# A hybrid decoder layer on one core: block pairs on unscaled operands, silu on ScalarE, fewer plain tiles, and a reordered last attention step

## The reference

```python
def rmsnorm(x, g):
    y = xf * lax.rsqrt(jnp.mean(xf * xf, axis=-1, keepdims=True) + RMS_EPS)
    return y * g

def swiglu(x, w_gate, w_up, w_down):            # D_MODEL 1024, D_FF 2816
    return (jax.nn.silu(x @ w_gate) * (x @ w_up)) @ w_down

h = h + 0.5 * swiglu(rmsnorm(h, ffn1_norm), ffn1_w_gate, ffn1_w_up, ffn1_w_down)
u = rmsnorm(h, mix_norm)
proj = u @ w_in        # pool input, q (16 heads of 64), k, v (2 heads), two gates
branch_pool = causal_pool_mixer(xp, pool_w, pool_scale) @ w_pool_out
branch_attn = sliding_window_sink_attention(q, k, v, q_norm, k_norm, sinks) @ w_attn_out
h = h + (gate_pool * branch_pool + gate_attn * branch_attn) @ w_out
h = h + 0.5 * swiglu(rmsnorm(h, ffn2_norm), ffn2_w_gate, ffn2_w_up, ffn2_w_down)
```

## Time and profile before

| what | value |
|---|---|
| median of 3 runs | 1023.11 us (1022.58 to 1025.37) |
| profiled execution, its own time | 1023.9 us |
| profiled execution, span from first to last instruction | 1022.1 us |
| granted TensorE clock, mean | 0.998 of full |
| busy: PE, PE weight load, DVE, ACT, POOL | 1015.0, 903.1, 758.1, 506.1, 309.9 us |
| matmuls | 6164 |

### The profile page before, as it was taken

How to read it: one execution, slowest core, us unless ns; L and a number is a source line. 1 busy time by engine, 2 the same in 40 slices (tenths; PEclk the granted TensorE clock), 3 DMA queues, 4 the chain that set the end, 5 groups by cost and what they waited for, 6 DMA issues and landing times.

```text
span 1022.1 us, 15961 instructions
## 1 busy us (share of the span) xinstructions
PE 1015.0 (99%) x6164; PEld 903.1 (88%) x6164; DVE 758.1 (74%) x1157; ACT 506.1 (50%) x878; POOL 309.9 (30%) x192
## 2 busy tenths in 40 slices
PE   9999999999999999999999999999999999999998
PEld 7888999998989888778888878888899999988897
DVE  6998677569986688537788766769885776599763
ACT  6543555555533343447787733336254555465231
POOL 1300233421131453444454443520014233310311
PEclk9999999999999999999999999999999999999999
DMA  6734667713332442222211222316467677233333
GB/s 216 219 106 121 178 175 190 212 45 124 94 95 103 139 139 83 83 88 65 75 62 62 83 83 63 122 41 198 111 170 202 158 183 191 90 104 104 103 104 104
DMA packets 42296, 124.86 MB, mean 122 GB/s; under 512 B 4336, under 2 KB 5616, under 8 KB 42224
## 3 DMA queue, kind: packets, MB, share of 16 engines
q1 hardware_dynamic: 37616, 107.85, 32.7%
q0 software_dynamic: 4320, 15.73, 8.7%
q10 hardware_dynamic: 288, 0.29, 0.1%
HBM read 121.76 MB, written 2.10 MB: 121 GB/s over the span
## 4 chain that ended last, share of the span: by engine, by line
PE 96%; DVE 1%; ACT 1%; DMA 1%; SPq 0%; issue 0%; DVEq 0%; ACTq 0%
PE psum L663 18%; PE psum L665 18%; PE psum L664 18%; PE psum L773 10%; PE psum L775 10%; PE psum L774 10%; PE psum L936 3%; PE psum L935 3%; PE psum L934 3%; PE psum L1090 1%; DMA h<-x_dram 1%; DVE sum_of_squares L1900 1%; PE psum L1120 1%; PE psum L1103 1%; PE psum L1121 1%
## 5 line engine op out<-in xcount | busy, mean ns | idle before, releaser
L1193 ACT ACTIVATE w_high<-w_raw 128x1024 fp32r<-128x1024 f32 x118 | 124.5, 1055 | 162.9 <-DMA w_raw<-weights_dram 113.8
L1757 POOL TENSOR_TENSOR w_low<-w_raw,w_high 128x1024 fp32r<-128x1024 f32 x50 | 122.9, 2462 | 116.5 <-ACT w_high L1193 95.5
L1757 POOL TENSOR_TENSOR w_low_in_place<-w_raw,w_high 128x1024 fp32r<-128x1024 f32 x27 | 66.4, 2461 | 196.9 <-ACT w_high L1193 196.9
L663 PE MATMUL psum<-u_high,w_high 128*128 128x512 f32 x240 | 96.9, 404 | 0.0
L665 PE MATMUL psum<-u_high,w_low 128*128 128x512 f32 x240 | 93.7, 391 | 0.0
L664 PE MATMUL psum<-u_low,w_high 128*128 128x512 f32 x240 | 93.5, 390 | 0.0
L663 PE MATMUL psum<-ffn_u_high,w_high 128*128 128x512 f32 x222 | 86.6, 390 | 0.0
L663 PE MATMUL psum<-hidden_high,w_high 128*128 128x512 f32 x222 | 86.5, 389 | 0.0
L664 PE MATMUL psum<-hidden_low,w_high 128*128 128x512 f32 x222 | 86.5, 389 | 0.0
L665 PE MATMUL psum<-ffn_u_high,w_low_in_place 128*128 128x512 f32 x222 | 86.4, 389 | 0.0
L664 PE MATMUL psum<-ffn_u_low,w_high 128*128 128x512 f32 x222 | 86.4, 389 | 0.0
(11 more groups left out here) (346 smaller groups left out, 3201.3 us busy)
## 6 DMA issues: line engine op xcount, KB each, us to landing
w_raw<-weights_dram SPq DMA_DIRECT2D x118, 512.0 KB, 3.5
gate_a<-weights_dram SPq DMA_DIRECT2D x15, 512.0 KB, 6.2
gate_s<-weights_dram SPq DMA_DIRECT2D x15, 512.0 KB, 3.7
gate_s<-weights_dram POOLq DMA_DIRECT2D x15, 512.0 KB, 6.4
up_a<-weights_dram SPq DMA_DIRECT2D x15, 512.0 KB, 4.7
up_s<-weights_dram SPq DMA_DIRECT2D x15, 512.0 KB, 3.6
up_s<-weights_dram POOLq DMA_DIRECT2D x15, 512.0 KB, 8.4
gate_a<-weights_dram SPq DMA_DIRECT2D x15, 256.0 KB, 5.2
```

Of the source, the lines that this page charges most:

```text
L663: pe.matmul(o, wh, xh, start=start, stop=False)
L1193: act.activation(high[:, s, :], raw[:, s, :], ACT.Copy).then_inc(high_done, 1)
L1757: pool.tensor_tensor(wlow[:, s, :], raw[:, s, :], high[:, s, :], ALU.subtract).then_inc(low_done, 1)
```

## The change

Four edits.

1. `PLAIN` goes from `(8, 6)` to `(6, 4)`: 6 plain tiles and 8 pairs in the first FFN, 4 and 9 in the second. The DMA of the first pair's weights is issued at other plain units.
2. The pairs work on unscaled operands. Four of the seven moving operands are now slices of the high and low parts that the plain tiles use, so their copies disappear; ACT makes `h * gain` in float32 (`unscaled`) and DVE the four sums from it (`sum_moving`). In return the results of a pair are multiplied by `rinv` on DVE: three instructions per pair that take gate and up together (`both`).
3. silu is one ACT instruction in place of tanh on ACT and two multiplications on DVE. The factor 0.25 of the residuals becomes 0.5.
4. In attention's last step DVE and ACT do `turned_part` of the last step ahead of `attn_part` of the step before it, and ACT does `small_part` ahead of the gate. POOL's last `low_part` waits for another semaphore.

```diff
-PLAIN = (8, 6)
+PLAIN = (6, 4)
-SUM_BANK = (1, 4, 3)
+SUM_BANK = (1, 4, 1)
...
+            def unscaled(n, c):
+                act.activation(ub[:, c:c + 1, :], h[:, c:c + 1, :], ACT.Identity, scale=at(gains[2 * n], c)
+                               ).then_inc(u_scaled, 1)
...
@@ ACT, pair @@
-                act.wait_ge(part_summed, 6 * g + 4)
-                act.activation(th[:, 0, :], gate_t[:, 0, :], ACT.Tanh, scale=0.5).then_inc(pair_tanh, 1)
+                act.wait_ge(pair_scaled, 3 * g + 1)
+                act.activation(gate_t[:, 1, right], gate_t[:, 1, right], ACT.Silu, scale=-1.0).then_inc(pair_silu, 1)
+                act.wait_ge(pair_scaled, 3 * g + 2)
+                act.activation(gate_t[:, 0, :], gate_t[:, 0, :], ACT.Silu).then_inc(pair_silu, 1)
                 if more:
                     high_s2(g + 1, up_w)
                     act.wait_ge(product, done(n, i, 10))
                     high_s31(g + 1, up_w)
-                act.activation(th[:, 1, right], gate_t[:, 1, right], ACT.Tanh, scale=-0.5).then_inc(pair_tanh, 1)
-                act.wait_ge(product, done(n, i, 12))
-                act.activation(th[:, 1, left], psum[:, x, left], ACT.Tanh, scale=-0.5).then_inc(pair_tanh, 1)
+                act.wait_ge(pair_scaled, 3 * g + 3)
+                act.activation(gate_t[:, 1, left], gate_t[:, 1, left], ACT.Silu, scale=-1.0).then_inc(pair_silu, 1)
...
@@ DVE, second_tile (the wait and the two multiplications by tanh are gone) @@
+                dve.wait_ge(product, done(n, i, 13))
+                dve.tensor_tensor(both[:, :, 1, left], psum[:, x:x + 2, left], two_of(rinv[:, left]), ALU.mult
+                                  ).then_inc(pair_scaled, 1)
...
@@ DVE, pair @@
                 add_part(up[:, 1, right], x + 1, 10, 6)
+                dve.wait_ge(part_summed, 6 * g + 5)
+                dve.tensor_tensor(both[:, :, 1, right], both[:, :, 1, right], two_of(rinv[:, right]), ALU.mult
+                                  ).then_inc(pair_scaled, 1)
                 add_part(up[:, 0, right], 7, 11, 5)
+                dve.wait_ge(part_summed, 6 * g + 6)
+                dve.tensor_tensor(both[:, :, 0, :], both[:, :, 0, :], two_of(rinv[:, :]), ALU.mult
+                                  ).then_inc(pair_scaled, 1)
                 if more:
                     low_s2(g + 1, up_w)
                     low_s31(g + 1, up_w)
-                dve.wait_ge(pair_tanh, 3 * g + 1)
-                dve.scalar_tensor_tensor(out=gate_t[:, 0, :], in0=th[:, 0, :], scalar=1.0, in1=gate_t[:, 0, :],
-                                         op0=ALU.add, op1=ALU.mult).then_inc(pair_silu, 1)
...
+                dve.wait_ge(pair_silu, 3 * g + 2)
                 dve.tensor_tensor(hid[:, f, :], gate_t[:, 0, :], up[:, 0, :], ALU.mult).then_inc(pair_hidden, 1)
...
@@ POOL @@
-                    pool.wait_ge(attn_low, 4 * NB)
+                    pool.wait_ge(pt_low, turned_lows(nb, j) + 3)
                     low_part(U_GATE + SLOTS + SLOTS * nb + j, j)
...
@@ DVE, norm: the sums of the moving blocks stand between its parts @@
+            norm_split(2)
+            sum_moving(1, NT2)
+            norm_variance(2)
+            sum_moving(1, T3)
+            norm_root(2)
```

More of the change, by code:

```diff
@@ L135 @@
 NEW1, NEW3, NEW2, NEW4 = range(4)
-B21, B22, B11, B12 = range(4)
-NT2, NT1, T3, T4 = range(4)
+B11, B12, B21, B22 = ((kh, half) for kh in range(2) for half in range(2))
+NT1, NT2, T3, T4 = range(4)
 def layer_kernel(nc, x_in, consts_in, params_in, poolw_in, weights_in, out):
@@ L1314, in plain @@
                     next_unit(base + 5)
-                    gate_tanh_tile(1, F)
-                    block_high(n, B22)
+                    gate_silu_tile(3, F)
                     next_unit(base + 6)
+                    high_a1(g, gate_w)
+                    high_s2(g, gate_w)
                     next_unit(base + 7)
-                    gate_tanh_tile(2, F)
-                    next_unit(base + 8)
-                    for t, count in sums[0]:
-                        sum_high(n, t, count)
@@ L1529, in _ @@
                 square(0, c, c)
+            for c in range(HALF):
+                unscaled(0, c)
             high_of_sum(0)
@@ L1742, in _ @@
                     square(2, c, c)
+                    unscaled(1, c)
             high_of_sum(2)
@@ L1907, in residual_of @@
             def residual_of(c):
[L1908 removed]
+                return dve.scalar_tensor_tensor(out=tile(h, c), in0=psum[:, c, :], scalar=0.5, in1=tile(h, c),
                                                 op0=ALU.mult, op1=ALU.add)
@@ L2055, in plain @@
+                    plain_tile(1)
                     weight_sums(g, gate_w)
                     low_a1(g, gate_w)
+                    unit_low(base + 6)
+                    sum_low(n, T3)
+                    sum_low(n, T4)
+                    low_s2(g, gate_w)
+                    unit_low(base + 7)
+                    low_s31(g, gate_w)
+                    plain_tile(2)
+                else:
+                    plain_scaled(n, base, 0, F)
+                    unit_low(base + 7)
+                    plain_scaled(n, base, 1, F)
+                    sum_moving(n, NT2)
+                    plain_hidden(0, F)
+                    plain_hidden(1, F)
+                    sum_moving(n, T3)
+                    sum_moving(n, T4)
+                    unit_low(base + 8)
+                    plain_scaled(n, base, 2, F)
+                    sum_low(n, NT1)
+                    sum_low(n, NT2)
+                    plain_hidden(2, F)
```

302 lines of the change are left out of this document (120 added, 182 removed).

## The result

The changed kernel takes **1031.87 us** (median of six executions, 1030.20 to 1034.33) against 1023.48 for the kernel before (six executions, 1022.58 to 1026.24). The ratio is 1.0079, with a 95% interval of 1.0059 to 1.0098: 0.8% slower, and 1.9 us above the predicted 1030.0. The profiled execution is the shortest of the six, 1030.2 us with a span of 1028.4 us, 6.3 us longer than the span of before.

The account below looks back on a forecast made before the run. The prediction took PE (busy 1015.0 of 1022.1 us) as the bound. From the profiled 1023.9: - 3.2 (PE work) - 3.8 (attention) + 13.9 (pairs' loop) = 1030.8, median 0.8 lower: 1030.0 us; range 1015.5 to 1035.

Parts of the forecast that it names:

- The work on PE, -3.2: In each FFN, two plain tiles (21.76 us) become one pair (20.16 us): 2 x 1.60 = 3.2 us less.
- The attention, -3.8: At the attention's end, the reorder removes PE's 2.14 us wait and slow matmuls behind it: 3.8 us less.
- A + 9.5 for the copy: In a pair, ACT's copy for the next pair's product 4 starts 9.5 us after A, the third add's start.
- The loop of 21.3: In the pairs, add, scalings, silu, copy, POOL, sums and next add close in 21.3 us against PE's 20.16; chance 0.58.
- the first sum now ends at A + 16.1, and from its end to the next third add are 5.23: In a pair, DVE's first weight sum ends behind POOL's rows, 16.1 us after the third add; 5.23 us of DVE work follow.
- the issue order: In the pairs, DVE's first sum may slip in ahead of POOL's last row, shortening the loop by about 0.1 us.
- Pair 0 has A = start + 16.1 in FFN 1: In FFN 1, pair 0's third add starts 16.1 us after the pair's start; in FFN 2, 14.9.
- the prediction's own formula: Last pair's product 4: 16.1 + 6 x 21.3 + 9.9 against 7 x 20.16 + 5.7 in FFN 1; FFN 2 likewise.
- 13.9: Total time lost to the loop in the pairs, in us: 7.0 in FFN 1 and 6.9 in FFN 2.
- The rival of the clock: In the pairs, the loop's waits also lower the clock: 22 us more, 1052 us, held unlikely; part of it 0.05.
- The plain parts at nothing: In the plain parts, plain matmuls cover the added DVE and ACT work: no cost, otherwise up to 1.2 us or twice that per FFN.

Follow-up runs that it names:

- Experiment 1: Changed kernel with ScalarE's rounding of the up weights' s2 and s31 moved ahead of the two silus within a pair; 1024.60 us.
- experiment 5: Changed kernel with GpSimd's four rows per pair copying the high part instead of subtracting, which makes those low parts wrong; 1024.11 us.
- experiment 6: Changed kernel with a pair's second scaling cut from 1024 to 32 elements a partition, so the first tile's results are not scaled; 1020.52 us.
- experiment 4: Changed kernel with two extra copies of h on ScalarE ahead of the first product's copy, in each pair but an FFN's first; 1041.98 us.
- Experiment 3: Changed kernel with ScalarE's rounding of the second down weights moved from behind to ahead of the last pair's last silu; 1026.79 us.
- experiment 8: Changed kernel with both ScalarE orders, those of Experiment 1 and Experiment 3, together; 1018.66 us.
- experiment 2: Changed kernel with ScalarE's rounding of s4 and a22 moved ahead of a pair's last silu, so GpSimd's four rows start earlier; 1035.06 us.

## Why the prediction was right, and where it was off

- **The result and its main cause: right.** The loop through scalings, silu, copy, POOL and the sums closes above PE's 20.16, and this makes the kernel slower. Experiments 1, 5 and 6 each shorten one member of it, on three different engines, and nearly all of the slip goes; experiment 4 lengthens it, and the slip grows with 0.77 of the delay.
- **The work on PE, -3.2: right** to 0.1 (21.75 and 21.76 for the plain tiles).
- **The attention, -3.8: right** in the stage (3.84) and by undoing it (418.52) or doing it alone (414.68). By the medians it is 3.0 and 3.5; the 1.7 us of it that are the clock are lost in only some executions.
- **A + 9.5 for the copy: right** (9.48), with silu at 0.63 and the scalings where they were put.
- **The loop of 21.3: mis-sized.** The step that failed is "the first sum now ends at A + 16.1, and from its end to the next third add are 5.23". POOL's last row is indeed the bound, but it holds the *second* sum: the first slips in ahead of it. The second ends at A + 16.5 with 4.5 to go: 21.0, not 21.3. In every second or third pair more of the sums slips in earlier, and the pair takes 20.7. I had allowed 0.1 for the issue order; it is 0.3 to 0.6.
- **When the loop takes hold: mis-sized.** "Pair 0 has A = start + 16.1 in FFN 1" came from the kernel before. Measured, the third add of pair 0 is 11.75 behind the issue of its `gate_a`, start + 14.8, so FFN 1 lost only what a loop entered 1.3 later loses. With 14.8 and third adds that stand 21.01 and 21.05 apart on average in the two FFNs, the prediction's own formula gives 4.0 and 5.1 us, the measured 9.1 in place of **13.9**.
- **The down projections: missed, +5.1.** The sum ended with the last pair's product 4. In a pair I had followed what stands behind each instruction that now waits longer, but not for the last silu of the *last* pair: behind it on ACT stand the second down weights, and ahead of what it waits for stand four low parts on DVE. Experiment 3 shows it. The two errors nearly cancelled (-4.8 and +5.1): that the time came out within 1.9 us is luck, though the direction is not.
- **The rival of the clock** did not come true in the pairs: the short waits left it at 1.00. It came true at the unforeseen waits, in some executions: three of the six lost clock, and the profiles of the other kernels with the same two waits place the fall there.
- **The plain parts at nothing: right.** No wait stands there.

Left open: why POOL's rows and the sums interleave in a way that repeats every two pairs in one FFN and less regularly in the other. The landing of `gate_a` varies (DVE's first sum starts 4.9 to 7.6 us behind its issue in these traces), and that was not controlled. In the changed kernel the one distance of 21.29 stands behind the latest landing.

## What to carry to other kernels

When an edit lets an instruction wait for something later than before, list what stands behind it on its engine at *every* place of the program, the last pass of the loop above all: the costlier wait here was outside the stage that was changed. A loop over engines that closes 4% above the bound engine's own pace costs in each pass, and one order on an engine with idle time can open it: ScalarE was 51% busy, and moving two roundings ahead of two silus that waited anyway brought 9.0 us in the pairs, 7.3 in the median. When undoing an edit to price it, undo it on all engines: VectorE's part alone gave 1.3 of 3.0 us.

## What the runs showed of the hardware

- **A wait of 2.1 to 2.3 us makes TensorE's clock fall in some executions and not in others; waits of up to 1.5 us never did.** The 38 executions of the five kernels whose longest wait is 1.5 us or less (experiments 3, 6, 8, and the two with the attention's edit in the kernel before) all have a mean granted clock of 1.000. Of the kernel before, with one wait of 2.1, 22 of 54 executions have 1.000 and a median of 1022.64 us, 32 have 0.998 and 1024.37: 1.7 us for one fall. Experiment 1, with two waits of 2.3, never reached 1.000 in 11 executions (0.997 or 0.998), and its windows show the lower level, 1.2 of 2.4 GHz for part of six microseconds. Experiments 2, 4 and 5 have the same two waits and 1.000 in one of 21 executions; the changed kernel has them and 1.000 in three of six. The profiles show the place: 16 waits of 2.1 to 2.3 us stand in eight profiled executions, the clock fell behind nine of them, and nowhere else while matmuls ran. The start of a down projection takes 32.01 to 32.12 us with a fall and 30.45 to 30.49 without, 1.6 us. What decides between the two is not shown.
- **The hold between GpSimd and VectorE moves with the order.** The row that is late is stretched, POOL's from 1.29 to 1.8 and DVE's from 0.69 to 1.8, and starting GpSimd 3.2 us earlier only moved the cost from the second sum to a product and the halves behind it (experiment 2).
